# A two-layer diffusion backbone on one core: conv and gate projections begun inside the last two scan turns, decay and rate products issued in pairs, and a scan block that carries two products

## The reference, cut to what matters

```python
hx = modulate(rms_norm(x, norm1_g[l]), sh1, sc1)      # same for the context
zx = hx @ w_in[l]                                     # all branches and gates
# A: RWKV-7, both directions, 16 heads of 64, per token
sa = einsum('bhvk,bhk->bhv', S, kk_t)
S = S * w_t - sa * kka_t + v_t * k_t;  y = S @ r_t
# decay w_t and rate a_t: z[..., 64 columns per direction] @ w_up[d], @ a_up[d]
# B: u = z[:, :512] * sigmoid(z[:, 512:1024]); depthwise conv, 31 taps; LayerNorm; swish; proj
# C: z = gelu(z); u, v = halves; u * (W_s LN(v) + b); proj
m = sum_i sigmoid(g_i) * branch_i;  x = x + gate1 * (m @ w_o)
x = x + gate2 * swiglu(modulate(rms_norm(x), sh2, sc2))
```

## Time and profile before

| what | us |
|---|---|
| median of 3 runs (4465.52 to 4477.34) | 4474.88 |
| the profiled execution | 4475.39 |
| its span | 4473.6 |
| layer 0: pair turns 0 and 1 | 92.6 to 256.2 |
| layer 0: turns 2 to 7 | 256.2 to 945.7 |
| layer 0: turn 8, turn 9 | 98.0, 16.9 |
| layer 0: branch list up to smean | 1060.6 to 1249.6 |
| layer 1: turns 2 to 7 | 2714.6 to 3378.6 |
| layer 1: turn 8, turn 9 | 95.5, 10.2 |
| layer 1: branch list up to smean | 3484.3 to 3624.7 |

### The profile page before, as it was taken

How to read it: one execution, slowest core, us unless ns; L and a number is a source line. 1 busy time by engine, 2 the same in 40 slices (tenths; PEclk the granted TensorE clock), 3 DMA queues, 4 the chain that set the end, 5 groups by cost and what they waited for, 6 DMA issues and landing times. The chain is left out here.

```text
span 4473.6 us, 108758 instructions
## 1 busy us (share of the span) xinstructions
PE 4219.4 (94%) x51156; PEld 2514.7 (56%) x51156; DVE 1365.3 (31%) x2121; ACT 1074.1 (24%) x1778; POOL 58.1 (1%) x52
## 2 busy tenths in 40 slices
PE   7999999988999999999999989999997899999998
PEld 3566666665555555555555556666666344444443
DVE  1555555554730000100000255555554220010000
ACT  2444444442020000100000244444443120010000
POOL 0000000000000000000000000000000000000000
PEclk8999999988999999999999989999998999999999
DMA  5000000003431111111111200000000532222222
GB/s 187 23 8 23 23 22 23 27 20 125 135 124 52 52 49 52 42 52 52 52 52 52 84 23 8 22 21 22 21 31 13 199 111 76 78 68 75 75 80 75
DMA packets 67388, 260.42 MB, mean 58 GB/s; under 512 B 7680, under 2 KB 9984, under 8 KB 66048
## 3 DMA queue, kind: packets, MB, share of 16 engines
q1 hardware_dynamic: 62208, 219.18, 15.4%
q10 hardware_dynamic: 3456, 29.04, 1.6%
q0 software_dynamic: 1280, 5.24, 0.3%
HBM read 239.80 MB, written 13.63 MB: 57 GB/s over the span
## 5 line engine op out<-in xcount | busy, mean ns | idle before, releaser
L584 PE MATMUL psum<-arena,ring 128*128 128x512 f32 (+1 forms) x4992 | 1805.0, 523 | 29.4 <-ACT arena L1326 22.6
L584 PEld LDWEIGHTS psum<-arena,ring 128*128 128x128 f32 x4992 | 950.5, 191 | 890.0 <-issue 816.0
L879 PE MATMUL psum<-arena 32*32 32x32 f32 (+4 forms) x40512 | 835.0, 212 | 147.0 <-issue 112.0
L879 PEld LDWEIGHTS psum<-arena 32*32 32x32 f32 (+3 forms) x40512 | 753.4, 122 | 336.8 <-issue 269.4
L766 PE MATMUL psum<-arena,ring 128*128 128x512 f32 (+1 forms) x1408 | 554.3, 523 | 2.5 <-ACT arena L1419 1.6
L1254 PE MATMUL psum<-arena,ring 128*128 128x512 f32 (+1 forms) x1440 | 520.2, 521 | 0.0
L1254 PEld LDWEIGHTS psum<-arena,ring 128*128 128x128 f32 x1440 | 273.6, 190 | 242.0 <-issue 229.6
L766 PEld LDWEIGHTS psum<-arena,ring 128*128 128x128 f32 x1408 | 254.2, 194 | 201.6 <-issue 178.3
L2161 DVE TENSOR_TENSOR arena<-psum,arena 128x768 f32<-128x768 f32 (+1 forms) x44 | 36.3, 825 | 718.8 <-PE psum L584 718.8
L2102 DVE TENSOR_TENSOR arena<-psum,arena 128x768 f32<-128x768 f32 (+1 forms) x48 | 39.6, 825 | 617.9 <-PE psum L584 617.9
L1698 ACT ACTIVATE arena<-psum 128x768 f32<-128x768 f32 (+1 forms) x44 | 31.0, 704 | 698.8 <-PE psum L584 698.8
(11 more groups left out here) (131 smaller groups left out, 2464.2 us busy)
## 6 DMA issues: line engine op xcount, KB each, us to landing
ring<-w_stream_in SPq DMA_DIRECT2D x408, 512.0 KB, 3.7
x_spill<-arena ACTq DMA_DIRECT2D x2, 3072.0 KB, 8.7
arena<-ya_spill ACTq DMA_DIRECT2D x2, 3072.0 KB, 10.0
arena<-x_spill ACTq DMA_DIRECT2D x2, 3072.0 KB, 18.5
ring<-w_stream_in ACTq DMA_DIRECT2D x8, 512.0 KB, 6.3
arena<-x_in ACTq DMA_DIRECT2D x1, 3072.0 KB, 14.3
arena<-ups_in SPq DMA_DIRECT2D x16, 192.0 KB, 2.4
ya_spill<-arena POOLq DMA_DIRECT2D x8, 384.0 KB, 6.8
```

The lines of the kernel that those rows point to most:

```text
L584: mm = eng.matmul(psum[0:lhs[k].shape[-1], tile, a - off:b - off], lhsT=lhs[k], rhs=rhs[k][:, a:b], start=(k == 0), stop=(k == len(lhs) - ...
L879: return pe.matmul(out, lhsT=lhs, rhs=rhs, start=start, stop=stop, skip_group_check=True)
```

## The change

- **Early branch work.** cb0, ca0, cb1, ca1 are projected in turn 8 (`early_tiles`, in the places of k, r, v and behind them), with sigmoid, product and 18 (layer 0) or 15 (layer 1) taps of conv 0 on ACT and DVE. su0, su1, su2 are projected in turn 9 (`gelu_tiles`), with their gelus; DVE does the rest of conv 0, and in layer 1 all 15 taps of conv 1. Turns 8 and 9 get their own weave strings; all other strings are new too.
- **The branch list** then has nine projections with three items behind each, ten behind smean; behind svar eleven in layer 0 and none in layer 1, where five are left for smean.
- **Pairs.** `up_tiles` issues both directions of a decay or rate product together, 512 tokens each and then 256 tokens each, into banks 0 and 1; they stand together instead of between the k- and r-tiles.
- **Key side.** The scaled keys of both directions lie side by side by chunk, so 12 transposes of 128 x 128 take the place of 24 matmuls.
- **z beside w.** Each w block also issues the z products of its group into another bank; ACT stores z behind w. The blocks stand w0 w1 u0 w2 u1 g0 u2.
- **Start.** ACT copies the modulation third ahead of the norm's factor, DVE does `mod_ready(0)` ahead of `normed`.
- Slots of the branch stage are renumbered.

```diff
-UP_ORDER = ((0, 0), (1, 1), (1, 0), (0, 1))
+UP_ORDER = ((0, 0), (1, 0), (0, 1), (1, 1))
-LANDS = dict(mean=(1, 1), bonus=(1, 0), lw=(0, 0, 0, 1), la=(1, 1, 0, 0), kkn=(0, 0), var=(1, 1), gu=(0, 0))
-BLOCKS = ["w0", "u0", "w1", "u1", "g0", "w2", "u2", "g1", "g2"]
+LANDS = dict(mean=(1, 1), bonus=(1, 0), lw=(0, 1, 0, 1), la=(0, 1, 0, 1), kkn=(0, 0), var=(1, 1), gu=(0, 0))
+BLOCKS = ["w0", "w1", "u0", "w2", "u1", "g0", "u2", "g1", "g2"]
...
+WEAVE.update((("PE", 0, t), "sdddddddddddddddddddddddsddddddsddddddssddddddddddddds") for t in (KT + 1,))
...
+EARLY, GELU_EARLY = ("cb0", "ca0", "cb1", "ca1"), ("su0", "su1", "su2")
...
-    for name in ("cb0", "ca0", "cb1", "ca1", "cb2", "su0", "su1", "su2", "su3", "ca2", "cb3", "sv0", "ca3", "sv1", "sv2", "sv3"):
-        entry(name, 2)
-    entry("smean", 8)
-    entry("svar", 8)
+    for name in ("cb2", "ca2", "cb3", "su3", "ca3", "sv0", "sv1", "sv2", "sv3"):
+        entry(name, 3)
+    entry("smean", 10)
+    entry("svar", 11)
...
+LAST_TURN_TAPS = ((18, 0), (15, 15))
...
+                def early_tiles(n, j, k0, k1):
+                    if not wanted(j):
+                        return
+                    a, b = HALVES[j]
+                    w = chunk_blocks(n)
+                    for k in range(k0, k1):
+                        if k == 0:
+                            hold(j, (eu if n % 2 else eg).at(l, 2 * (n // 2) + j))
+                            arrived(pe, f"branch{l}", n)
+                        mm = pe.matmul(bank(j, z=b - a), lhsT=w[k], rhs=hs[k][:, a:b], start=(k == 0), stop=(k == KT - 1))
+                        if k == KT - 1:
+                            mm.then_inc(early.sem, 2 if l == DEPTH - 1 else 1)
+                        yield
+                def gelu_tiles():
+                    S = phases[f"branch{l}"]["PE"]
+                    pe.wait_ge(*yv.at(KT * (l + 1) - 1))
+                    for n, name in enumerate(GELU_EARLY):
+                        q = len(EARLY) + n
+                        tile = branch_tiles(l)[name]
+                        arrived(pe, f"branch{l}", q)
+                        if n == 2:
+                            pe.wait_ge(*phases[f"branch{l}"]["A"].at("su0"))
+                        for a, b in halves(y0, y0):
+                            for k, w in enumerate(chunk_blocks(q)):
+                                mm = pe.matmul(psum[:, tile, a - y0:b - y0], lhsT=w, rhs=hs[k][:, a:b], start=(k == 0), stop=(k == KT - 1),
+                                               skip_group_check=True)
...
+                        a, b = HALVES[i]
+                        for d in DIRS:
+                            assert UP_ORDER[2 * i + d] == (d, i) and LANDS[name][2 * i + d] == d
+                            hold(d, reader.at(g, 2 * i + d))
+                        for d in DIRS:
+                            pe.matmul(bank(d, z=b - a), lhsT=ups_block(g, n, side(d)), rhs=slot(src)[side(d)][:, a:b],
+                                      start=True, stop=True).then_inc(ev.sem, 1)
...
+                    yield from k_tiles(t, 1, 2, 8)
+                    yield from decay_tiles(t, 0)
+                    yield from decay_tiles(t, 1)
+                    yield from rate_tiles(t, 0)
+                    yield from rate_tiles(t, 1)
+                    yield from r_tiles(t, 0, 0, 8)
...
-                            a = ((k - 10) * GRP + n) * C
-                            for d in DIRS:
-                                mm = mm64(bank(b, side(d), n * P, n * P + P), slot(kr(g, d, 0), a, a + C), ident, True, True)
-                            continue
+                            a = kr(g, 0, 0) * T + ((k - 10) * GRP + n) * P
+                            src = arena[:, a:a + P]
                         mm = pe.transpose(bank(b, a=n * P, z=n * P + P), src, ident)
...
+                                if kind == "w":
+                                    for d in DIRS:
+                                        rows = side(1 - d)
+                                        mz = mm64(bank(z_bank(i), side(d), at, at + HD), pcols(d, h, c, 0, C, rows), tok(UV, d, c, rows, a, z), True, True)
...
-                norm_rsqrt(0, 2, 0)
                 act.wait_ge(*S.at(f"m0.{MOD_ITEMS - 1}"))
                 mod_copy(0)
+                norm_rsqrt(0, 2, 0)
```

369 lines of the change are left out of this document (205 added, 164 removed).

## The result

The changed kernel takes 4495.7 us (median of 6 runs, 4491.4 to 4497.8), the kernel before 4474.6 (6 runs beside them): a ratio of 1.0041, 95% interval 1.0031 to 1.0051. It is slower by 0.4%; the forecast was 4351, faster by 2.8%, with a range from 4295 to 4430. The profiled execution took 4495.8 (span 4494.0), 20.4 more than the one of before.

The account below looks back on a forecast made before the run. PE, busy 94% of the span, was taken as the bound. Start -6.4, turn 0 +2, turns 1 to 7 -98, turn 8 +19.6, turn 9 +34.5, branch lists -44 and -32: -124.3 from 4475.4, 4351 us, range 4295 to 4430.

Parts of the forecast that it names:

- The work removed per turn: Steady turns: pairs save 3.3 us, returns 0.4, keys 1.4, z 3.0, in sum 8.1 us a turn.
- What of it shows: Turns 1 to 7: 8 us a turn taken in layer 0, 6 in layer 1, together -98 us.
- My own sign of being wrong: Steady turns staying above 110 us in layer 0, or PE waiting at the pairs.
- The four points: Turn 8 and steady turns, both layers: up to some 97 us of work a third shows, above it three quarters.
- Turn 8: Turn 8 with added projections: +14.6 us in layer 0, +5 in layer 1, +19.6 in all.
- Branch list: Branch list with smean and svar: -44 us in layer 0, -32 in layer 1, waits for weights included.
- The reload: Gap ahead of ca2: 11 us in layer 0, 12.7 in layer 1; equal queue turns would give some 5.
- (e): Pairs: PE waits for empty banks, 12.7 us a turn, 178 in all, 4529 us; chance 0.07.
- (b): Pairs and z: tiles do not overlap, 4386 us, with the quadrants too 4428; chance 0.07.
- (a): Turns: the scan's chain bounds them, so they give 62 us, 4387 us; chance 0.15.
- (d): Turns: half of the waits go too, 4 us a turn more, 4295 us; chance 0.12.
- (c): Branch lists: the clock falls in each gap, 48 us where 10 were counted, 4389 us; chance 0.09.

Follow-up runs that it names:

- wide products: Each scan burst issues 24 32x64 products instead of 48 matmuls, values wrong: 4252.1 us on the kernel before, 4231.2 on the changed one.
- the repaired kernel: Changed kernel with spread layer 0 string, two items behind each projection, six items earlier, earlier DVE centring, later ACT copy: 4430.3 us, ratio 0.9894.
- the kernel with two items: Changed kernel with two modulation items instead of three behind each branch-list projection, the rest behind smean and svar: 4480.9 us, ratio 1.0012.

## Why the prediction was wrong, point by point

- **Start, turn 9:** right. -6.2 for -6.4; 37.4 and 23.3 us for 36.6 and 25. No wait of over 0.9 us stayed in the tail.
- **The work removed per turn:** right. The sum of the prices was 8.1 us. With wide products, where next to no stalls cover it, PE is busy 96.7 us instead of 103.1, and at that clock (0.98 of 102.2 us, about 2 us lost) some 8 us of work are gone. The keys alone gave 1.5 us for 1.4. Pairs did overlap: the rows of after have pairs of 512 and 256 tokens at 1.06 and 0.63 us between starts (two others of the same turn, at the low clock, at 1.20 and 1.15), and w with z of group 0, 64 passes, takes 1.09:

```profile
638.98 1.13 PE L897 MATMUL psum<-arena 64*128 64x512 f32 x4
640.04 0.77 PE L948 MATMUL psum<-arena 32*32 32x32 f32 x67
...
641.91 0.70 PE L897 MATMUL psum<-arena 64*128 64x256 f32 x4
642.54 1.00 PE L948 MATMUL psum<-arena 32*32 32x32 f32 x94
...
669.72 1.16 PE L948 MATMUL psum<-arena 64*64 64x64 f32 x64
670.81 1.98 PE L834 MATMUL psum<-arena,ring 128*128 128x512 f32 x4
```

- **What of it shows:** this is the step that failed, -98 us for which +14 came. I wrote that in layer 0 "the turn is bound by PE", and counted a us of work as a us of turn; I put the waits that the new order would add at nothing. My own sign of being wrong came with it: the six turns of layer 0 are 116.3 us on average, above 110. The six turns of layer 0 together say where it went, per turn: busy -5.6, stalls at "issue" +4.6 (28.7 us in six turns before, 56.1 after), waits with a name +2.6 (none before, 15.4 us after), in sum +1.6 for the +1.4 measured. In layer 1: busy -3.9, "issue" +5.9 (35.2 us in six turns before, 70.6 after), waits with a name -1.1 (15.5 and 8.7), in sum +0.9 for +0.9. Busy time fell by less than the work since more of it ran at 1.2 GHz. So most of the loss is the supply's, and in layer 0 about a third of what came back are waits that the new order brought; with wide bursts these are 5.2 us a turn.
- **The four points,** by which the turn's length followed work with a slope of a third below 97 us, and which I laid to the scan's chain, were read wrongly. The flat part was mostly the supply. Turn 8 of before had 16.0 us of "issue" waits and a clock of 0.81; with wide bursts it is 75.5 us instead of 98.0, with 2.2 us of them, and 9.2 us of waits for DVE and ACT (5.8 before):

```profile
PE psum L879 <- issue: 16.0, 10, 2.4
```

```profile
PE psum L879 <- issue: 2.2, 4, 1.0
```

- **Turn 8:** +20.2 and +18.8 for +14.6 and +5. The work was well sized (104.8 forecast; 106.5 busy at a clock of 0.97, 103 without the 3.5 that the clock costs; in layer 1 85.2 and 83). What failed is the rest: 7.8 us of waits and clock in layer 0 became 15, and in layer 1, which I took from the points, 31 instead of 15: 20.8 us idle and a clock of 0.91. The waits at "issue" did fall there, from 16.0 and 18.0 to 6.1 and 14.4 us, those with a name are 4.5 and 5.5, and the clock costs 3.5 and 10.3. That layer 1 has more of them fits its having fewer tiles to stand between the same 864 burst matmuls; no run tests it.
- **Branch list:** the list itself came out at 140.5 and 107.1, which is -48.5 and -33.2 for -50.7 and -31.8 with the clock's 5. The long waits were 10.1 and 11.0 us for 11 and 12.7, the short ones 1.9 for 1.9. Smean to the first gate was +12.2 for +6.5 in layer 0: ten items behind smean took 15.0 us and eleven behind svar 15.7, 1.4 to 1.5 us each for the 1.3 that I took. In layer 1, +9.9 for 0: "its five late items fall into a wait that is there now" is false. The rows show why:

```profile
3642.81 1.05 PE L721 MATMUL psum<-ring,arena 128*32 128x512 f32 x4 [0.33 <-DMA ring<-w_stream_in]
3646.72 6.50 PE L613 MATMUL psum<-arena,const 128*128 128x512 f32 x8 [2.86 <-ACT arena L1727]
```

The last item ends at 3643.9. ACT copies that third and only then makes the squares (L1727) for which svar waits, since the copy stands ahead of them in its order. That is the 2.9 us of wait. The other 7 of the 9.9 are the items, which take 5.7 us where the old wait was 3.3, and longer products and waits behind them. In the repaired kernel the copy stands behind and the items are shared out anew, and this stretch is 24.4 us instead of 36.0; how much of it is the copy's was not measured.
- **The reload:** the two long waits say again that a chunk took 12 and 13 us beside the 7 MB on ACT's queue. The earlier trace rows had disagreed with equal halves, and so do these; but halves were my reading. The Trainium skill (DMA: Bandwidth & Descriptors, Queues, rings and completion order) has the turns by packet, and packets differ in size. In the kernel before, from 3498 to 3504 us (ACT's queue, then that of the weights: packets, MB, share):

```profile
q10 hardware_dynamic: 90, 2.21, 85.5%
q1 hardware_dynamic: 89, 0.36, 14.7%
```

The packets are equal in number, but 24.6 and 4.0 KB long, so the chunk gets a seventh of the bytes. The trace agrees with the page's rule, and with it the long waits were to be expected.
- **Rivals.** (e) named a price of the right kind, waits at the pairs, but of 1.5 us in a turn instead of 12.7, and hardly visible before the supply is out of the way (1.7 us in six turns). (b) is refuted: the tiles overlap. (a) gave 4387 for a chain that did not bind in layer 0 and took 2.6 us a turn in layer 1. (d) went the other way: waits did not halve, they rose. (c) was near in kind: the clock of the steady turns and of the list fell (0.97 to 0.94, 0.99 to 0.94), as the stalls and the waits grew. None of them named the supply of instructions, though its mark stood in the earlier trace rows as "issue": the profile named no engine for these four us, and I did not ask what they were.

## What to carry to other kernels

Where PE's stalls are named "issue" and fall inside bursts of small matmuls, count the instructions from one stall to the next before pricing anything: if it is always the same number, work removed elsewhere may not show (here the keys' did in layer 0, the rest did not), and the lever is fewer instructions, or long tiles placed between the bursts. An order that takes fillers away from one stretch to cover waits in another has a price in the stretch it takes them from. And when a stage gets shorter, ask of each engine whether it is still early: here DVE's centring (14 us in the kernel with two items) and ACT's copy (2.9) took back part of what the moved work had given.

## What the runs showed of the hardware

- PE's program comes in packets of 16 KB, 256 instructions, 3.45 to 4.0 us apart at best (once 6.5), some 70 instructions in a us. A burst of 32x32 float32 matmuls asks for 192 in 0.95 us. The Trainium skill (Runtime: NRT & Kernel Launch, Instruction fetch mechanics) has the blocks of 256 instructions and says that the cost of crossing a boundary is "mostly hidden". The trace agrees with the block and disagrees with the hiding: 28.7 us of stalls in six turns of the kernel before, 56.1 in the changed one. By its rule, as an estimate from these sums, there would be no such stalls and the turns of layer 0 would be about 5 us (before) and 9 us (after) shorter.
- Half of the burst's instructions less, with the same area written, is worth 222 us of 4474 (5%), about a quarter of it the bursts' own time, and more than any change of the case. It was one execution, but the times of the kernel before spread over 27 us only. A form of the scan's levels that gives right values with fewer, larger products was not tried.
- Executions of the kernel before with full bursts differ by up to 4 us from turn to turn; with wide ones its six turns of layer 0 agree to 0.1 us. So the spread from turn to turn is the supply's and the clock's; whether that from execution to execution is too was not measured.
- Two DMA queues with work took turns packet by packet: 90 packets of 24.6 KB beside 89 of 4.0 KB in 6 us.
